# Gated linear attention in a decoder kernel: half-wide level products, two heads per matmul, one masked copy per level, a norm by tile

## The reference

```python
def gla_chunked(q, k, v, log_a):          # cut; chunks of 16 tokens
    q = q * dk ** -0.5
    b = jnp.cumsum(log_a, axis=3)
    decay = jnp.exp(jnp.where(causal[:, :, None], diff, NEG_INF))      # diff = b_i - b_j
    scores = jnp.einsum('bhnid,bhnjd,bhnijd->bhnij', q, k, decay)
    o_intra = jnp.einsum('bhnij,bhnjv->bhniv', scores, v)
    ...                                   # a scan carries the state over chunks
    return (o_intra + o_inter)
...
    oc = rms_norm(oc, gla_g).astype(x.dtype) * jax.nn.silu(gc)
```

## Time and profile before

| | us |
|---|---|
| median of 3 runs | 1877.17 (1876.15 to 1878.55) |
| the profiled execution, its time | 1874.99 |
| its span, first to last instruction | 1873.2 |
| PE busy | 1777.7 |
| DVE busy | 1303.8 |
| ACT busy | 979.8 |
| POOL busy | 13.8 |

### The profile page before, as it was taken

The page is one execution under the profiler, slowest core; times in us unless marked ns, Lnnn a source line. Parts: engine busy times, 40 slices in busy tenths (PEclk is TensorE's granted clock), DMA queues, the critical chain, the costliest instruction groups (busy, mean ns, idle before and its releaser), DMA issues.

```text
span 1873.2 us, 21553 instructions
## 1 busy us (share of the span) xinstructions
PE 1777.7 (95%) x7962; PEld 1390.5 (74%) x7962; DVE 1303.8 (70%) x1217; ACT 979.8 (52%) x861; POOL 13.8 (1%) x22
## 2 busy tenths in 40 slices
PE   7999998999989998888999999999999999999996
PEld 6846674788867465747788888888888888888885
DVE  5464544445454554445988989889899898898996
ACT  4333122344233331314767767777677777776773
POOL 0000000000000000000000000000000000000000
PEclk9998799999999988997999999999999999999998
DMA  8523052454545231346999999999999999999991
GB/s 288 180 90 112 22 181 90 164 184 170 178 160 180 90 112 61 120 143 233 349 366 347 367 342 364 369 347 361 345 360 371 344 360 359 355 364 342 365 359 63
DMA packets 206471, 466.19 MB, mean 249 GB/s; under 512 B 11952, under 2 KB 14416, under 8 KB 206416
## 3 DMA queue, kind: packets, MB, share of 16 engines
q1 hardware_dynamic: 200880, 463.76, 68.9%
q10 hardware_dynamic: 5536, 1.68, 0.4%
HBM read 464.36 MB, written 1.05 MB: 248 GB/s over the span
## 4 chain that ended last, share of the span: by engine, by line
PE 90%; DVE 6%; ACT 2%; issue 1%; DMA 1%; POOL 0%; ACTq 0%; DVEq 0%; SPq 0%
PE ps L1427 22%; PE ps L1823 16%; PE ps L1825 16%; PE ps L1824 16%; PE ps L1454 6%; PE ps L1745 3%; PE ps L1803 2%; PE ps L1812 1%; PE ps L1618 1%; DVE w_lo L871 1%; PE ps L1388 1%; PE ps L1671 1%; PE ps L1653 1%; PE ps L1537 1%; PE ps L1580 1%
## 5 line engine op out<-in xcount | busy, mean ns | idle before, releaser
L871 DVE TENSOR_TENSOR w_lo<-ring,w_hi 128x2048 fp32r<-128x2048 f32 x336 | 767.7, 2289 | 120.5 <-ACT w_hi L556 117.5
L556 ACT CAST w_hi<-ring 128x2048 fp32r<-128x2048 f32 x336 | 641.9, 1911 | 280.1 <-PE ps L1825 265.1
L1823 PE MATMUL ps<-w_hi,xe_hi 128*128 128x512 f32 x896 | 353.2, 394 | 3.2 <-DVE w_lo L871 1.8
L1825 PE MATMUL ps<-w_hi,xe_lo 128*128 128x512 f32 x896 | 349.3, 390 | 0.0
L1824 PE MATMUL ps<-w_lo,xe_hi 128*128 128x512 f32 x896 | 348.7, 389 | 0.0
L1823 PEld LDWEIGHTS ps<-w_hi,xe_hi 128*128 128x128 f32 x896 | 168.2, 188 | 38.7 <-DVE w_lo L871 2.7
L1825 PEld LDWEIGHTS ps<-w_hi,xe_lo 128*128 128x128 f32 x896 | 168.1, 188 | 35.8
L1824 PEld LDWEIGHTS ps<-w_lo,xe_hi 128*128 128x128 f32 x896 | 168.4, 188 | 33.8
L1823 PE MATMUL ps<-w_hi,he_hi 128*128 128x512 f32 x448 | 178.2, 398 | 0.0
L1825 PE MATMUL ps<-w_hi,he_lo 128*128 128x512 f32 x448 | 174.8, 390 | 0.0
L1824 PE MATMUL ps<-w_lo,he_hi 128*128 128x512 f32 x448 | 174.4, 389 | 0.0
(11 more groups left out here) (260 smaller groups left out, 1846.1 us busy)
## 6 DMA issues: line engine op xcount, KB each, us to landing
ring<-in_moe_w_dram SPq DMA_DIRECT2D x336, 1024.0 KB, 5.5
ring<-in_ffd_w_dram SPq DMA_DIRECT2D x31, 1024.0 KB, 5.0
ring<-in_w_in_dram SPq DMA_DIRECT2D x24, 1024.0 KB, 5.5
ring<-in_xa_wkv_dram SPq DMA_DIRECT2D x16, 1024.0 KB, 5.0
ring<-in_w_out_dram SPq DMA_DIRECT2D x8, 1024.0 KB, 5.0
ring<-in_xa_wq_dram SPq DMA_DIRECT2D x8, 1024.0 KB, 4.9
ring<-in_xa_wo_dram SPq DMA_DIRECT2D x8, 1024.0 KB, 5.1
ring<-in_ffd_w_dram SPq DMA_DIRECT2D x4, 512.0 KB, 3.6
```

The lines of the kernel that those rows point to most:

```text
L556: act.copy(w_hi[:, q % SPLIT_SLOTS, :], ring[:, q % RAW_SLOTS, :]).then_inc(hi_ready, 1)
L871: dve.tensor_tensor(w_lo[:, q % SPLIT_SLOTS, :], ring[:, q % RAW_SLOTS, :], w_hi[:, q % SPLIT_SLOTS, :].bitcast(F32), ALU.subtract).then_i ...
L1823: pe.matmul(ps[:, bank, :], x_hi, hi[:, c, cols], start=first, stop=False)
L1825: return pe.matmul(ps[:, bank, :], x_lo, hi[:, c, cols], start=False, stop=last)
```

## The change

- `products(s)` multiplies only what the level uses: the queries of the upper halves and the keys of the lower halves, 256 elements each instead of 512. The queries are written by two instructions, one for partitions 0 to 63 and one for 64 to 127, into a layout in which each block has 64 columns for the pair's first head and 64 for its second; the other head's rows in those columns stay zero. The keys stay in place.
- The zeros are written by POOL, over a whole half of `qk` (1024 elements per partition): `clear(1)` after `dec_diff` (the last `level_exponents`), `clear(0)` after `pv_done`. `products(1)` and `products(2)` wait for them (`zeros_ready`).
- At levels 1 to 7 PE makes 4 matmuls instead of 8, one for each block, with 128 rows and 128 columns: both heads at once. They go to one bank, 5 for odd s and 7 for even s (`level_bank`).
- `combine(s)` has one masked copy of 512 elements (8 x 64) for a level; `st` and `stx` are laid out by block, then head. The mask has 64 columns per level instead of 128.
- Step 8's scores go to banks 4 and 6, and ACT, instead of DVE's `combine(8)`, copies them to `stx`. PE waits for that (`cross_taken`) before tile 1's output only.
- `gla_out`, the square, the sum and the power are done for each tile. DVE's copy of the memory keys stands between the two tiles' sums.
- POOL multiplies the gate by `g_c` in place, one instruction of 384 elements for each tile, after the Silu and, in POOL's order, before `clear(0)`. DVE's L1111 goes.

```diff
-    level = np.zeros((P, LEVELS, P), np.int32)
+    level = np.zeros((P, LEVELS, P // 2), np.int32)
     for v in range(LEVELS):
         half = (P // 2) >> v
         block = i // (2 * half)
-        upper = (i // half) % 2
-        level[:, v, :] = (block[:, None] == block[None, :]) & (upper[:, None] == 0) & (upper[None, :] == 1)
+        lower = (i // half) % 2 == 0
+        level[:, v, :] = (block[:, None] == block[~lower][None, :]) & lower[:, None]
...
+            def clear(parity):
+
+                pool.memset(qk[:, parity, :, :], 0.0).then_inc(zeros_ready, 1)
+
+            def power(k, c):
+
                 pool.wait_ge(var_ready, k + 1)
                 pool.tensor_tensor(rstd[:, c], var[:, c], mhalf[:, c], ALU.pow).then_inc(rstd_ready, 1)
+
+            for l in range(DEPTH):
+                pool.wait_ge(dec_diff, l + 1)
+                clear(1)
+                power(POWERS * l, slice(0, 8))
+                pool.wait_ge(gate_silu, l + 1)
+                for t in range(T):
+                    gate = h[:, t, C_G:C_RANK].rearrange("p (h k) -> p h k", h=CH)
+                    pool.tensor_tensor(gate, gate, g_c[:, l, :].unsqueeze(1).to_broadcast([P, CH, CV]), ALU.mult)\
+                        .then_inc(gate_scaled, 1)
+                pool.wait_ge(pv_done, UNITS * (l + 1))
+                clear(0)
+                for t in range(T):
+                    power(POWERS * l + 1 + t, slice(4 * t, 4 * t + 4))
+                for n in range(3 * T):
+                    power(POWERS * l + 3 + n, slice(n % T, n % T + 1))
...
-                act.wait_ge(gla_out, l + 1)
-                act.activation(zz[:, 0:2, :], ps[:, 2:4, 0:CH * CV], ACT.Square).then_inc(gla_square, 1)
+                act.wait_ge(level_scores, GSTEPS * (l + 1))
+                for hp in range(2):
+                    act.copy(stx[:, :, hp, :], ps[:, 4 + 2 * hp, 0:S].rearrange("p (b s) -> p b s", b=2))\
+                        .then_inc(cross_taken, 1)
+                for t in range(T):
+                    act.wait_ge(gla_out, T * l + t + 1)
+                    act.activation(zz[:, t, :], ps[:, 2 + t, 0:CH * CV], ACT.Square).then_inc(gla_square, 1)
...
                 def products(s):
 
-                    if s >= 3:
+                    half = P if s > LEVELS else P >> s
+                    qs, ks = (qk_all[:, 2 * S * n:2 * S * (n + 1)].rearrange("p (m w) -> p m w", w=2 * half) for n in range(2))
+                    ds = dec[:, s - 1, :].rearrange("p (m w) -> p m w", w=2 * half)
+                    upper, lower = slice(half, 2 * half), slice(0, half)
+                    if s <= 2:
+                        dve.wait_ge(zeros_ready, 2 * l + s)
+                    else:
                         dve.wait_ge(level_scores, GSTEPS * l + s - 1)
-                    for n in range(2):
-                        ins = dve.tensor_tensor(qk[:, s % 2, n, :], tr[:, 10 + 2 * n:12 + 2 * n, :].rearrange("p b s -> p (b s)"),
-                                                dec[:, s - 1, :], ALU.mult)
-                    ins.then_inc(level_ready, 1)
+                    if s <= LEVELS:
+                        into = qk[:, s % 2, 0, :].rearrange("p (b h n i) -> p b h n i", b=4, h=2, i=half)
+                        for hp in range(2):
+                            r = slice(64 * hp, 64 * hp + 64)
+                            q4, d4 = (v[r, :, upper].rearrange("p (b n) i -> p b n i", b=4) for v in (qs, ds))
+                            dve.tensor_tensor(into[r, :, hp], q4, d4, ALU.mult)
+                    else:
+                        dve.tensor_tensor(qk[:, s % 2, 0, 0:S].rearrange("p (m i) -> p m i", i=half), qs[:, :, upper],
+                                          ds[:, :, upper], ALU.mult)
+                    dve.tensor_tensor(qk[:, s % 2, 1, :].rearrange("p (m w) -> p m w", w=2 * half)[:, :, lower],
+                                      ks[:, :, lower], ds[:, :, lower], ALU.mult).then_inc(level_ready, 1)
 
                 def combine(s):
 
                     dve.wait_ge(level_scores, GSTEPS * l + s + 1)
-                    for hp in range(2):
-                        src = ps[:, 4 + 2 * hp + s % 2, :].rearrange("p (b q) -> p b q", b=4)
-                        if s == 0:
-                            ins = dve.tensor_tensor(st[:, hp], src, ident.unsqueeze(1).to_broadcast([P, 4, P]), ALU.mult)
-                        elif s <= LEVELS:
-                            ins = dve.copy_predicated(st[:, hp], level[:, s - 1, :].unsqueeze(1).to_broadcast([P, 4, P]), src)
-                        else:
-                            ins = dve.tensor_copy(stx[:, hp], src[:, 0:2, :])
+                    if s == 0:
+                        for hp in range(2):
+                            src = ps[:, 4 + 2 * hp, :].rearrange("p (b q) -> p b q", b=4)
+                            ins = dve.tensor_tensor(st[:, :, hp], src, ident.unsqueeze(1).to_broadcast([P, 4, P]), ALU.mult)
+                    else:
+                        half = P >> s
+                        n = P // (2 * half)
+                        into = st.rearrange("p b h (n w) -> p (b h) n w", n=n)[:, :, :, half:]
+                        mask = level[:, s - 1, :].rearrange("p (n i) -> p n i", n=n).unsqueeze(1).to_broadcast([P, 8, n, half])
+                        ins = dve.copy_predicated(into, mask,
+                                                  ps[:, level_bank(s), :].rearrange("p (m n i) -> p m n i", m=8, n=n))
                     done(ins)
                     dve.sem_inc(level_taken, 1)
...
-                for s in range(GSTEPS):
+                for s in range(LEVELS + 1):
                     if s + 2 < GSTEPS:
                         products(s + 2)
                     combine(s)
                     if s == 1:
                         dilated_output()
-                dve.wait_ge(gla_square, l + 1)
-                done(dve.tensor_reduce(var[:, :].rearrange("p (t h) -> p t h", t=T),
-                                       zz[:, 0:2, :].rearrange("p t (h k) -> p t h k", h=CH), AX, ALU.add))
-                norm_of(POWERS * l + 1, 8, CV, lambda: turn(TURN["k", l], kT))
-                dve.wait_ge(gate_silu, l + 1)
                 for t in range(T):
+                    dve.wait_ge(gla_square, T * l + t + 1)
+                    done(dve.tensor_reduce(var[:, 4 * t:4 * t + 4], zz[:, t, :].rearrange("p (h k) -> p h k", h=CH), AX, ALU.add))
+                    norm_of(slice(4 * t, 4 * t + 4), CV)
+                    if t == 0:
+                        turn(TURN["k", l], kT)
+                for t in range(T):
+                    dve.wait_ge(rstd_ready, POWERS * l + t + 2)
                     oc = o_tok[:, t, S + BH * BD:D].rearrange("p (h k) -> p h k", h=CH)
                     done(dve.tensor_tensor(oc, ps[:, 2 + t, 0:CH * CV].rearrange("p (h k) -> p h k", h=CH),
                                            rstd[:, 4 * t:4 * t + 4].unsqueeze(2).to_broadcast([P, CH, CV]), ALU.mult))
-                    done(dve.tensor_tensor(oc, oc, g_c[:, l, :].unsqueeze(1).to_broadcast([P, CH, CV]), ALU.mult))
                     oc = o_tok[:, t, S + BH * BD:D]
+                    dve.wait_ge(gate_scaled, T * l + t + 1)
                     done(dve.tensor_tensor(oc, oc, h[:, t, C_G:C_RANK], ALU.mult))
                     dve.sem_inc(mixed, 1)
...
-                        pe.wait_ge(level_taken, GSTEPS * l + s - 1)
-                    for hp in range(2):
+                        pe.wait_ge(level_taken, (LEVELS + 1) * l + s - 1)
+                    if s == 0:
                         for pair in range(2):
-                            for t in range(T if s <= LEVELS else 1):
+                            for t in range(T):
+                                b = 2 * pair + t
+                                at = slice(t * P, (t + 1) * P)
+                                for hp in range(2):
+                                    r = slice(64 * hp, 64 * hp + 64)
+                                    ins = pe.matmul(ps[:, 4 + 2 * hp, b * P:(b + 1) * P], tr[r, 12 + pair, at],
+                                                    tr[r, 10 + pair, at], start=True, stop=True)
+                    elif s <= LEVELS:
+                        for b in range(4):
+                            at = slice(b * P, (b + 1) * P)
+                            ins = pe.matmul(ps[:, level_bank(s), at], qk[:, s % 2, 1, at], qk[:, s % 2, 0, at],
+                                            start=True, stop=True)
+                    else:
+                        for pair in range(2):
+                            for hp in range(2):
                                 r = slice(64 * hp, 64 * hp + 64)
-                                if s == 0:
-                                    q, k = tr[r, 10 + pair, :], tr[r, 12 + pair, :]
-                                else:
-                                    q, k = (qk[r, s % 2, n, pair * S:(pair + 1) * S] for n in range(2))
```

(16 more changed lines are left out.)

27 lines of the change are left out of this document (14 added, 13 removed).

## The result

| | before | after |
|---|---|---|
| median of the runs made together, us | 1877.68 (1876.15 to 1878.55) | 1861.48 (1860.50 to 1862.41, 4 runs) |
| the profiled execution, its time / its span | 1874.99 / 1873.2 | 1860.50 / 1858.7 |

The ratio is 0.9915, 95% interval 0.9903 to 0.9927: 16.2 us faster by the medians, 14.5 by the two profiled executions. I had forecast 11.4.

A forecast was written before the change was run, and what follows sets the result against it. PE bounds the kernel, busy 95% of the span, but in this stage the chain changes hands. Savings of 4.6 - 0.5 + 0.8 + 0.8 = 5.7 us per layer, 11.4 in all, give 1863.6 profiled, 1865.8 median; range 1873 to 1860.5.

The forecast's parts named there:

- The reading of what bounds the stage: PE bounds the kernel, but in this stage the chain changes hands; in the levels DVE and PE are nearly level.
- The levels: Levels 2 to 7, at 2.08 us each, take 11.1 us in place of 15.7: 4.6 saved per layer.
- I take 0.72, the row's own: One masked copy of 512 elements per level, strided destination: 0.72 us, bounds 0.7 and the old pair's 1.25.
- The zeros: Before `products(2)`, which waits for POOL's `clear(0)` behind the two gate multiplies: 0.5 us lost per layer.
- my first rival: POOL's gate multiplies and DVE exclude each other, `clear(0)` ends 1.9 later: gain 3.8 per layer, 1869.6 us; chance 0.16.
- Step 8: Between `combine(7)` and the output's first record: PE's step 8 lies mostly beside `combine(7)`, saving 0.8 us.
- The output: PE's output after the levels: the same 24 records, 5.45 us, no gain.
- my fourth rival: 128-row matmuls bring full clock before the output's 24 records, saving up to 2.5 more per layer: 1860.8 us; chance 0.08.
- The norm: Output's end to out-projection, 9.55 us before: 9.6 at low clock, 7.9 at full clock; 0.8 saved, in between.
- The sum: Both layers' stages: 4.6 - 0.5 + 0.8 + 0.8 = 5.7 us saved per layer, 11.4 for both.
- it shifts along: What follows the stage is fed by slots the out-projection frees, so it moves earlier with the stage.
- What I said would prove me wrong: Longer products at s = 7 than at s = 1, late `clear(0)`, or a stage 5.7 us shorter without a shorter kernel.

The follow-up runs named there:

- the dense destination: Changed kernel with each level's masked copy writing its eight 64-column blocks in one run, scores landing in wrong columns: 1854.51 us, ratio 0.9887.
- the opposite edit: Changed kernel with each level's scores made by eight matmuls of 64 rows and 64 columns, and two masked copies of 256 elements: 1865.52 us, ratio 0.9939.
- the gate late: Changed kernel with POOL's gate multiplies moved behind the second clearing and the last masked copy, beside PE's output: 1858.41 us, ratio 0.9899.

## Why the prediction was right and wrong

**The reading of what bounds the stage** held: the chain changes hands, and a level is set by PE and DVE almost equally. Levels came every 2.05 to 2.14 (forecast 2.08), a round of eight 128-row records at 1.2 GHz took 2.04, and the three products 1.21 (forecast 1.18), at short runs no more than at long ones. From start to start they took 0.43, 0.43 and 0.34: two of three overlaps were lost, as charged.

**The levels** gave 4.0 for 4.6. The step that failed is "I take 0.72, the row's own", for the masked copy with a strided destination: right for five levels, 1.3 for two. I had kept the old pair's 1.25 as the bound for all levels at once, and had not asked where a stride could begin to cost. With the dense destination this part gains 0.61 more, the whole shortfall.

**The zeros** cost 1.1 for 0.5, and the step put the cost in the wrong place. `clear(0)` ended at 174.19 (forecast 174.55), and `products(2)` at 174.36 didn't wait for it; DVE was late itself, being held 0.8 and then 0.8 by POOL's multiplies. So my first rival was right in its mechanism and I gave it 0.16. The row with which I argued against it is a power of one element per partition; the rival itself named that weakness. My 0.95 for the multiply was near: alone it takes 1.00, beside DVE 1.17. Without the hold this part would even have gained: with the gate late it is 5.76 against 6.30. The rival's price was nevertheless wrong: it had the hold delay `clear(0)` by 1.9 and this part lose 2.4, where DVE's side was held and the part lost 1.1; and its total, 1869.6, also missed what the other terms gave.
The Trainium skill, SBUF — State Buffer, section "Who interferes with whom", says that a DVE instruction with two SBUF inputs contends with a GpSimd instruction that reads SBUF and not with one that only writes it, and that the shared port is an exclusive lock. These runs agree in all three: 1.22 for 0.42 beside the multiply, 0.76 for a pair beside the memset, and holds that shortened with POOL's instruction when the multiplies were halved. In the prediction I had let one narrow row speak against it.

**Step 8** gave 0.9 for 0.8.

**The output** gave 2.5 for 0. "The output itself is the same 24 records, 5.45" failed: the records are the same, the clock isn't. This was my fourth rival, at 0.08; the run that changes only the rows shows it (2.95), and the opposite edit bears it out (5.35). My argument against it, that the clock stayed low through 12 us of nearly unbroken records, was drawn from 64-row records alone, in a change that turns them into 128-row ones.

**The norm** gave 2.6 and 2.2 for 0.8. I had 0 with the clock low and 1.65 with it full. By the runs 1.2 and 1.5 are the two multiplies taken from DVE (gate back on DVE), 0.57 the split by tile (norm of both tiles together), and the rest the second eight transposes, 1.09 in layer 0 and 1.85 in layer 1 against 1.97. I counted the multiplies at their place in DVE's order and then, in the low-clock half of my mean, let the 16 transposes swallow them; with those at 1.76 they don't.

**The sum** came out 11.4 against 17.5 in the stages. Errors of -0.6 (zeros) and -0.6 (copies) stand against +2.5 (output) and +1.6 (norm) per layer. That the range held is luck in good part. Its far end was 8.3 per layer, and the stages gained 8.95 and 8.5; the bounds that made up that end were cheaper products, cheaper zeros and the clock in the norm, and the first two didn't come. The time stayed inside because part of the gain was lost outside the stages, where "it shifts along" failed: the lead shrank from 9.6 to 3.5 us between the two layers. The fourth rival's 1860.8 is within 0.7 of the measured median, nearer than the forecast's 1865.8, but by the same cancellation. What I said would prove me wrong came in part: the copies were not at 0.72 in all levels, and the output's first record came 3.9 earlier in the stage, not 5.

## What to carry to other kernels

Ask of each matmul group what clock it leaves to the next one: here the clock was low through the work that followed 64-row matmuls, and going back to 64 rows, with two copies per level, cost 2.4 us in that work and 1.9 ahead of it (layer 0). Before moving a two-input step to POOL, look at what DVE does at that moment; here the same step, put where DVE stood still, held nothing up. A price for an operation holds for the access pattern of its row: for a masked copy, look at the shortest run in the destination.

## What the hardware showed that I had not expected

- With all 128 rows in the level matmuls the granted clock was 1.00 over 172 to 204 us, with nothing else changed in a kernel that had 0.50 in 183 to 195 and 197 to 203; with 64 rows in the changed kernel it was 0.50 over 176 to 200. With 128 rows in the changed kernel it still fell, 0.50 over 176 to 188, and was full for the output in all but three of the stages traced.
- A masked copy of 512 elements takes 0.69 to 0.72 us down to runs of four elements in the destination, and 1.3 with runs of two and of one; a plain copy or a product with the same destination runs takes its usual time (1.52 for two copies, 0.42 for a product of 256).
- Beside POOL's multiply of 384 elements a two-input DVE instruction of 256 takes 1.22 in place of 0.42, and beside one of 192 elements 0.72 to 0.81; beside POOL's memset it isn't held.
